# Sums of squares added by VectorE in PSUM, the norm and the weight loads of the second part moved, and two token sums formed by GpSimd

## The reference

```python
x = x + rmsnorm(a, g_attn_post[layer])      # a: attention output times w_o
h = rmsnorm(x, g_ffn_pre[layer])
f = conv_ffn(h, ffn_w_up[layer], ffn_conv_w[layer], ffn_conv_b[layer], ffn_w_down[layer])
x = x + rmsnorm(f, g_ffn_post[layer])

def rmsnorm(x, g, eps=NORM_EPS):
    xf = x.astype(jnp.float32)
    y = xf * lax.rsqrt(jnp.mean(xf * xf, axis=-1, keepdims=True) + eps)
    return (y * g.astype(jnp.float32)).astype(x.dtype)

def conv_ffn(h, w_up, conv_w, conv_b, w_down):
    u = h @ w_up                             # 1024 x 5632
    u = lax.conv_general_dilated(...) + conv_b   # causal, 3 taps, per channel
    gate, val = jnp.split(u, 2, axis=-1)
    return (jax.nn.silu(gate) * val) @ w_down
```

## Time and profile before

| | us |
|---|---|
| median of 3 runs | 2676.34 (2675.14 to 2676.84) |
| the profiled execution, its time | 2680.91 |
| its span (first to last instruction) | 2679.1 |
| PE busy | 2487.5 (93%) |
| DVE busy | 1946.4 (73%) |
| POOL busy | 1520.2 (57%) |
| ACT busy | 850.1 (32%) |
| chain that ended last: PE, DVE, ACT | 76%, 13%, 4% |
| mean granted TensorE clock | 0.969 of full |

### The profile page before, as it was taken

The page is one execution under the profiler, slowest core; times in us unless marked ns, Lnnn a source line. Parts: engine busy times, 40 slices in busy tenths (PEclk is TensorE's granted clock), DMA queues, the critical chain, the costliest instruction groups (busy, mean ns, idle before and its releaser), DMA issues.

```text
span 2679.1 us, 31652 instructions
## 1 busy us (share of the span) xinstructions
PE 2487.5 (93%) x11964; PEld 1974.9 (74%) x11964; DVE 1946.4 (73%) x2185; ACT 850.1 (32%) x1441; POOL 1520.2 (57%) x1153
## 2 busy tenths in 40 slices
PE   6999999989999999996899999978989999999994
PEld 4788888767777777773577787767767777777772
DVE  4467666577888788889667676665677887888878
ACT  3245442342111111113346565652342111111112
POOL 4231123638888888884431323113538888888883
PEclk9999999999999999998899999988999999999997
DMA  3121215311111111113211212143211111111112
GB/s 134 48 70 65 79 56 212 110 63 48 51 52 60 50 47 48 56 40 148 66 49 47 66 53 87 33 157 118 103 63 48 56 57 54 48 48 56 51 60 110
DMA packets 51237, 191.98 MB, mean 72 GB/s; under 512 B 5904, under 2 KB 6416, under 8 KB 47376
## 3 DMA queue, kind: packets, MB, share of 16 engines
q1 hardware_dynamic: 39184, 148.92, 16.2%
q10 hardware_dynamic: 11904, 41.05, 4.0%
HBM read 146.43 MB, written 29.36 MB: 66 GB/s over the span
## 4 chain that ended last, share of the span: by engine, by line
PE 76%; DVE 13%; ACT 4%; issue 3%; DMA 2%; POOL 1%; SPq 1%; ACTq 0%; POOLq 0%; DVEq 0%
PE ps L1168 9%; PE ps L1169 9%; PE ps L1170 9%; PE ps L1190 6%; PE ps L1192 5%; PE ps L1191 5%; PE ps L1011 3%; PE ps L983 2%; PE ps L985 2%; PE ps L984 2%; PE ps L1101 2%; PE ps L1102 2%; PE ps L1103 2%; PE ps L1028 2%; PE ps L1048 2%
## 5 line engine op out<-in xcount | busy, mean ns | idle before, releaser
L1978 DVE TENSOR_TENSOR a<-a,ps 128x1024 f32<-128x1024 f32 x336 | 409.3, 1220 | 173.9 <-PE ps L1192 166.3
L733 POOL CAST w_hi<-w_raw 128x1024 fp32r<-128x1024 f32 x78 | 85.0, 1089 | 788.2 <-PE ps L985 274.3
L1524 ACT ACTIVATE cy<-cx,cv 128x1024 f32<-128x1024 f32 x80 | 99.7, 1247 | 706.5 <-DVE cx L1949 706.5
L815 POOL TENSOR_TENSOR ring<-w_raw,ring 128x512 fp32r<-128x512 f32 x208 | 301.7, 1450 | 16.6
L1190 PE MATMUL ps<-hid,ring 128*128 128x512 f32 x704 | 293.8, 417 | 13.1 <-DVE a L1978 13.1
L813 POOL CAST ring<-w_raw 128x512 fp32r<-128x512 f32 x208 | 183.2, 881 | 209.4 <-PE ps L1192 91.2
L1191 PE MATMUL ps<-hid,ring 128*128 128x512 f32 x704 | 276.8, 393 | 0.0
L1192 PE MATMUL ps<-hid,ring 128*128 128x512 f32 x704 | 276.8, 393 | 0.0
L1168 PE MATMUL ps<-h,ring 128*128 128x512 f32 x640 | 249.2, 389 | 0.0
L1169 PE MATMUL ps<-h,ring 128*128 128x512 f32 x640 | 249.0, 389 | 0.0
L1170 PE MATMUL ps<-h,ring 128*128 128x512 f32 x640 | 249.0, 389 | 0.0
(11 more groups left out here) (259 smaller groups left out, 6551.6 us busy)
## 6 DMA issues: line engine op xcount, KB each, us to landing
w_raw<-in_W SPq DMA_DIRECT2D x166, 512.0 KB, 3.2
raw_d<-in_W SPq DMA_DIRECT2D x44, 512.0 KB, 3.2
h<-o_dram ACTq DMA_DIRECT2D x2, 6144.0 KB, 20.8
x_dram<-x ACTq DMA_DIRECT2D x6, 2048.0 KB, 7.6
x<-x_dram SPq DMA_DIRECT2D x2, 4096.0 KB, 12.8
dsw<-draw SPq DMA_DIRECT2D x64, 128.0 KB, 2.3
o_dram<-most SPq DMA_DIRECT2D x6, 1024.0 KB, 4.1
o_dram<-dost SPq DMA_DIRECT2D x6, 1024.0 KB, 3.9
```

Of the source, the lines that this page charges most:

```text
L815: pool.tensor_tensor(lo, raw[name], hi.bitcast(F32), ALU.subtract).then_inc(item_ready, 1)
L1978: dve.tensor_tensor(a[:, f, :], a[:, f, :], src, ALU.add).then_inc(acc_done, 1)
```

## The change

The diff has six parts.

1. **Squares of `a`.** The adds of `add_square` write bank 7 and take it as an input; the first takes two squares, so that there are seven adds for a half and not eight, and only the last one writes `ss`. The memset of `ss` goes.
2. **Squares of `x`.** ACT writes the eight squares of a half to a tile of their own, `xq`. DVE adds squares 0 to 6 in bank 3 (`add_x_square`, six adds, behind `new_x` of the next tile), and PE sums over the partitions by two products, not eight.
3. **The places of PE's sums.** `x_sums` of the first half stands inside unit 12, after its fourth tile, and not after units 10, 11 and 12. `x_sums` of the second half stands ahead of the fifth tile of v0 of n = 1, and not at six places from the last tile of v0 of n = 0 on. `a_sum(1)` stands ahead of the fifth tile of the first g0, not the seventh, and the wait for the last copy and for `b_kept` goes from the head of g0.
4. **g1 and v1 of n = 0** run in turn, tile by tile.
5. **Loads.** The wait for `x_spilled` goes from the load of `raw_d`; POOL forms the weight sums of n = 2 ahead of item G2, not S2.
6. **Token sums.** POOL forms T3 and T4, behind item S1 and ahead of d1; DVE forms T1 ahead of its first conv tile and T2 ahead of the second. ACT's tops of T2 and T1 stand ahead of its taps of n = 1, and DVE's rests of T2 and T1 ahead of the conv tiles of n = 1.

```diff
         def added_bank(half, i):
-            return bank(((5, 7), (1, 3))[half][i % 2])
+            return bank((5, 1)[half])
+        def squares_of(half, k):
+            return half_of(xq, k // 2, k % 2)
...
                     if n >= 2:
                         sp.wait_ge(item_ready, item_count(layer, n - 2, "d2"))
-                    else:
-                        for spilled in x_spilled:
-                            sp.wait_ge(spilled, SPILLED[2 * layer + 1])
                     load_ffn(layer, n - 1, "D")
...
+                def token_sums(name):
+                    for k in range(KH):
+                        out, _, _ = combination(name, k)
+                        if name == "T3":
+                            pool.wait_ge(t_sum["T1"], KH * layer + k + 1)
+                            x0, x1 = half_of(a, KH + k, 1), half_of(a, k, 1)
+                        else:
+                            pool.wait_ge(t_sum["T2"], KH * layer + k + 1)
+                            x0, x1 = half_of(a, KH + k, 0), combination("T2", k)[0]
+                        pool.tensor_tensor(out, x0, x1, ALU.subtract).then_inc(t_sum[name], 1)
                 for n, name in ITEMS:
-                    if n >= PLAIN and name == ("S2" if n == PLAIN else "G1"):
+                    if n >= PLAIN and name == ("G2" if n == PLAIN else "G1"):
                         sums(n)
...
                     item(n, name)
+                    if (n, name) == (PLAIN, "S1"):
+                        token_sums("T3")
+                        token_sums("T4")
...
-            def x_sums(n, half, k0, k1):
...
+            def x_sums(layer, half):
+                pe.wait_ge(xq_add, (KT - 2) * (2 * layer + half + 1))
+                pe.matmul(bank(6 + half), ones[:, :], squares_of(half, KT - 2), start=True, stop=False).then_inc(b_stat, 1)
+                pe.wait_ge(x_sq, 16 * (2 * layer + 1) + KT * (half + 1))
+                pe.matmul(bank(6 + half), ones[:, :], squares_of(half, KT - 1), start=False, stop=True
+                          ).then_inc(b_stat, 1)
...
                         for k in range(KT):
+                            if (n, k) == (KT + 4, 4):
+                                x_sums(layer, 0)
                             wh, wl = blk(n % 2, k)
...
-                        elif n in (KT + 2, KT + 3):
-                            x_sums(2 * layer + 1, 0, 3 * (n - KT - 2), 3 * (n - KT - 1))
-                        elif n == KT + 4:
-                            x_sums(2 * layer + 1, 0, 6, KT)
...
+                def plain_units():
+                    pe.wait_ge(proj_out, CH[f"wo{layer}"] + U_WO - 1)
                     for k in range(KT):
-                        if (n, part, k) == (0, "g0", 6):
+                        if k == 4:
+                            pe.wait_ge(b_kept, KT * (layer + 1))
                             pe.wait_ge(b_lo, 2 * KT * layer + KT)
                             pe.wait_ge(ss_add, SS[2 * layer])
                             a_sum(1)
-                        if half == 0 and (n, v, k) in STAT_PLACES:
-                            x_sums(2 * layer + 1, 1, *STAT_PLACES[n, v, k])
...
+                        plain_part(0, "g0", k)
+                    for n, part in ((0, "v0"), (1, "g0"), (1, "v0")):
+                        for k in range(KT):
+                            if (n, part, k) == (1, "v0", 4):
+                                x_sums(layer, 1)
+                            plain_part(n, part, k)
+                    for k in range(KT):
+                        plain_part(0, "g1", k)
+                        plain_part(0, "v1", k)
+                    for part in ("g1", "v1"):
+                        for k in range(KT):
+                            plain_part(1, part, k)
...
                 def x_square(i):
-                    if i >= 2:
-                        act.wait_ge(x_stat, nx * 16 + i - 1)
-                    act.activation(half_of(sq, 0, i % 2), half_of(x, k, half), ACT.Square).then_inc(x_sq, 1)
+                    if half:
+                        act.wait_ge(b_stat, 4 * layer + 2)
+                    act.activation(squares_of(half, k), half_of(x, k, half), ACT.Square).then_inc(x_sq, 1)
...
-                square(KT + 4)
                 rstd_x(0)
                 for n, tiles_ in enumerate(((0, 1, 2), (3, 4, 5), (6, 7))):
+                    square(KT + 4 + n)
                     for i in tiles_:
                         block_parts(i)
-                    square(KT + 5 + n)
+                square(KT + 7)
...
                 gate_and_split(0)
+                sum_tops(layer, "T2")
+                sum_tops(layer, "T1")
...
                 tap(1, 1)
-                sum_tops(layer, "T2")
-                sum_tops(layer, "T1")
+                sum_tops(layer, "T3")
                 gate(1)
-                sum_tops(layer, "T3")
                 sum_tops(layer, "T4")
...
                 def add_square(n):
+                    half, t_ = n // KT, n % KT
+                    if t_ == 0:
+                        return
...
+                    dve.tensor_tensor(half_of(ss, 0, half) if t_ == KT - 1 else bank(7),
+                                      half_of(sq, 1, 0) if t_ == 1 else bank(7), half_of(sq, 1, n % 2), ALU.add
+                                      ).then_inc(ss_add, 1)
+                def add_x_square(half, k):
+                    if not 1 <= k <= KT - 2:
+                        return
...
+                    dve.tensor_tensor(squares_of(half, k) if k == KT - 2 else bank(3),
+                                      squares_of(half, 0) if k == 1 else bank(3), squares_of(half, k), ALU.add
+                                      ).then_inc(xq_add, 1)
                 def new_x(i):
...
-                    if k >= 2:
-                        dve.wait_ge(f_new, 16 * layer + i - 1)
+                    else:
+                        dve.wait_ge(f_new, 16 * layer + i)
...
+                    add_x_square(half, k - 1)
```

## The result

The changed kernel takes 2657.61 us (median of 4, 2655.32 to 2659.13), the kernel before, run beside it, 2676.36 (2675.14 to 2676.84): the ratio is 0.9932, with a 95% interval of 0.9916 to 0.9947. That is 18.7 us less, where 41.8 were forecast, and 1.6 us above the top of the range. The profiled execution took 2655.3 us, span 2653.5. Of the 25.6, 3.4 lie ahead of the first product of layer 0's output product, where the kernels are the same.

A forecast was written before the change was run, and what follows sets the result against it. PE bounds the kernel, with time won in its stops, extra work and low clock. Per layer -10.3 + 0.7 - 4.8 - 1.1 - 5.4 = -20.9 us, -41.8 in all: 2634.5 against 2676.3, range 2617 to 2656.

The forecast's parts named there:

- the twelve products: Norm: twelve of sixteen products with `ones` go in each layer, 0.86 us of PE each, -10.3 us.
- the adds with a PSUM operand: DVE's adds of squares in the norm: 0.69 us each, 0.61 from one to the next back to back.
- the head of the FFN: Around the first g0: 1.3 us of stop replaces 3.22 and 2.9 of slow clock, -4.8 us a layer.
- the second half: Norm of the second half, ahead of g1: 1.1 us of stop for 2.23, -1.1 us a layer.
- S to Z: From the output product's first product to the start of g1: 15.5 us less a layer.
- from g1 to the end of the first down product: FFN stretch expected to fall from 54.4 to 49 us, DVE and POOL overlapping partly: -5.4 us a layer.
- (b): DVE and POOL meet all the time from g1 on; stretch stays 53.9 us, -16 a layer, 2644 us; chance 0.20.
- x_sums of the first half: In unit 12 of the output product: short waits for DVE's adds, +0.7 us a layer (0 to 2).
- slow clock at the head of g0: Low PE clock after the 3.22 us stop there costs another 2.9 us a layer, which would go.
- (a): DVE and POOL hardly meet from g1 on; stretch is PE's 43.5 us, about -28 a layer, 2620; chance 0.20.
- (c): Norm: the new adds cost as much as the old ones; -8 us a layer, 2660; chance 0.10.
- (d): From g1 on GpSimd is starved, its sums taking 8.3 us each; +25 a layer net, 2727; chance 0.03.

The follow-up runs named there:

- one_column: The changed kernel with each of POOL's eight token sums cut to one column of 512; 2646.7 us, ratio 0.9900 to the kernel before.
- psum_first: The changed kernel with ACT writing the first square of each sum straight to PSUM; 2647.9 us, ratio 0.9899 to the kernel before.
- before_swap_first: The kernel before, with ACT's 6 MB reload in the second attention held behind the last swap; 2674.2 us, ratio 1.0000.
- pool_only: The kernel before with only T3 and T4 formed by POOL and the new orders of sums, tops and rests, norm unchanged; 2679.9 us, ratio 1.0029.
- norm_only: The changed kernel with T3 and T4 formed by DVE again and the old orders of the FFN's head; 2664.7 us, ratio 0.9964 to the kernel before.

## Why the prediction was wrong

**What held.** The place (one stretch in each layer), the twelve products, PE's gain of nothing by the freed DVE in the output product, the adds with a PSUM operand (0.61 forecast, 0.69 measured, back to back 0.60), the head of the FFN (0.32 us of stop where 1.3 stood, and no slow clock), the second half (0.36 us ahead of x_sums, 0.86 ahead of g1 for the forecast 1.1). S to Z came out at -14.5 and -11.9, forecast -15.5, in this pair of traces; what other traces say of it stands below.

**The failed step: from g1 to the end of the first down product, -5.4 us a layer; measured +0.3 and -0.5.** The frame was right (DVE's conv tiles of n = 1 and then 11.2 us to P7), the two prices were right (four rests 2.5 alone, 5.5 to 6.2 beside POOL), how long the dear one holds was not: the overlap was mis-sized, in two steps. First, the 49 us do not follow from my own terms. With POOL at work from Z + 10.2 everything up to T2's rests is dear, which puts their end at Z + 33.2; T1's rests are then done at Z + 35.7 if POOL stops at 32, and at about 38 if it stops at 37, and the stretch ends at 50.8 to about 53. That is -1.5 to -3.6 us, not -5.4. Second, POOL was to be done with "eight sums and three items more" at Z + 32 to 37, but beside DVE its own work grows as well: the sums ran from Z + 17.2 to 30.5 (1.49 and 1.86 us each), and d1, d2 and S3 took 8.1 us for 5.8, until Z + 38.7. V2, the next d1 and a weight sum followed without a gap, until Z + 44.2, but only the end of the last rest meets them. So all eight rests of T2 and T1 (Z + 27.7 to 39.2) lie beside POOL. In this stretch rival (b), given 0.20, is what happened: conv ends at Z + 44.2, which that rival's sum had at 44.0. Its total of 2644 missed too, by 13.6 us, for the reasons below. one_column shows the size: 5.3 us a layer hang on the eight sums, and another part on the splits.

**A mis-sized term: x_sums of the first half, +0.7 us; measured 2.66.** The sum priced all six adds at 0.61, and named in the same breath that one of six has both operands in SBUF. The first add of the x squares cost 2.19, that of the second half of `a`, which stands ahead of x_sums in DVE's order, 1.55, where the sum had "two copies and an add 1.8". psum_first shows what they are worth: 2.36 us of stop a layer, 6.4 us in the median of the kernel.

The Trainium skill (SBUF — State Buffer, section "Who interferes with whom") makes this very distinction, one SBUF input against two beside GpSimd; the rows of the changed kernel (2.19 and 0.69, 3.5 us apart) and of psum_first (0.69 in the same place) agree with it. Beside each of the three an instruction of POOL that reads SBUF was running.

**Not in the prediction: the swap, +5.1 us.** That attention is not touched is true of the code only. No row of the kernel before speaks of it but the wait of 0.94 us for a transfer, with a 6 MB transfer issued 0.3 us behind it by another queue.

**The base.** I took 2.9 us a layer of slow clock at the head of g0 as certain. Windows behind that stop, of the kernel before and of before_swap_first, whose code is the same there:

```profile
522.88:539.88 17.00, 13.78 (x47) 10.44 (x46) 7.66 (x12) 4.62 (x9) 10.23 (x11) 0.80 0.10 36
```

```profile
522.47:539.47 17.00, 13.77 (x56) 10.25 (x55) 10.43 (x16) 5.29 (x10) 10.42 (x11) 1.00 0.10 34
```

Behind the same stop of 3.2 us the mean granted clock was 0.80 in one execution and 1.00 in the other, and S to Z is 133.9 there and 131.1 here. With layer 1 and pool_only there are six such stretches: three at 1.00, two at 0.90, one at 0.80. The first page was also that of an execution above the median (2680.9, 2676.3). So a part of those 2.9 us a layer was no gain to be had on average.

Together: 10.6 (the stretch) + 6.4 (first adds) + 5.1 (swap) = 22.1 of the 23.1 us between forecast and result. That the three fill it so well is partly luck, since the base was too high as well. Means over all traces in which a stretch has the code of before (two or three) or of the changed kernel (seven to nine) give the same picture from another side: S to Z 11.6 and 11.9 us less for the forecast 15.5, which misses 7.5; Z to P7 the same and 0.5 less for 5.4 each, which misses 10.4; P7 to S 7.0 us more where VectorE waits long for the swap (1215.0 in eight traces, 1208.0 in the three with the old norm). That is 24.9 for 23.1.

**The rivals.** (a) falls by the same rows. (c) is right for the one add in six that has both operands in SBUF (2.19 us), and with it came a stop of 2.66 us; the other five cost 0.69. (d) fell: POOL's sums took 1.49 and 1.86 us, and no stop of PE waits for d1. But the starved cast is there again in norm_only, DVE's row first:

```profile
593.69 4.89 DVE L1977 TENSOR_TENSOR x_r<-a,x_r 128x512 fp32r<-128x512 f32 x8
```

```profile
592.02 8.18 POOL L817 CAST ring<-w_raw 128x512 fp32r<-128x512 f32 x1 [13.97 <-PE ps L1197]
```

## What to carry to other kernels

Before work is moved to a second engine, write down everything that this engine does in the same window, behind the moved work too, price both engines' instructions for the whole overlap, and follow the sum to its end: here the eight sums pushed three weight items beside VectorE's rests, and these took 8.1 us for 5.8. Price each instruction of a chain by its own operands, above all the first, which often starts from two tiles in SBUF. And a part that makes PE faster should be judged with the order of the engine that PE waits for next: the same norm part (with its loads) was worth 10 us with the old order (ratio 0.9964) and 22 to 26 with the new (2679.9 to 2657.6; 1.0029 to 0.9932).

## What the hardware showed unexpectedly

- A DVE add with both operands in SBUF that begins inside an instruction of POOL ends 0.55 to 0.57 us behind it (five cases in the changed kernel: 2.19 and 1.55 us in both layers and once 0.92, for 0.69). In long trains both engines lose: DVE's sum 1.29 and rest 1.54 us for 0.62, POOL's sum 1.49 to 1.86 (a weight sum took 1.30). But in norm_only a cast of POOL begun at 592.02 stood for 8.18 us, while DVE ran T4's sums, eight rests and a product back to back at full speed (rests 0.61 each), and ended 0.5 us behind the last of them. Why one train shares and the other doesn't was not tried.
- One DMA issue of SyncE that took 1.3 us instead of 0.6, with an instruction packet moving just ahead of it, turned the order of two queues and cost 5 us, because the other queue's next transfer was 6 MB. Holding back the large transfer, which nothing needed soon, by 2 to 3 us takes the risk away at no cost that could be measured (before_swap_first, 1.0000).
- After a stop of PE of 3.2 us the granted clock falls in some executions and not in others (means of 0.80, 0.90 and 1.00 over the next 17 us, from 3.8 us ahead of g0 on, for the same instructions).
